# Whole output columns in the last four weight blocks of the first experts, and sums of squares by a matrix of ones

## The chip, the cores and the metric

The kernel runs on one core of one Trainium2 chip. The metric is the device time of one execution in microseconds (us). In the profile PE is the engine of the matmuls and PEld its weight loads, DVE, ACT and POOL are the vector, scalar and GpSimd engines, and SP is the engine that issues the DMAs. All data are 32-bit floats.

## What is computed

The reference is a block with a gated linear attention, a long convolution and a mixture of 16 experts, and two further layers behind it. The part around the change is the end of the first mixture of experts and the norm behind it:

```
hid = silu(xs @ w_gate) * (xs @ w_up)              # per expert, 32 slots of 1024
y   = (hid @ w_down) * vals
x   = x + mod_x[5] * zeros.at[idx].add(y)          # 256 rows of 1024
x   = x * rsqrt(mean(x * x, -1) + 1e-6) * norm_final_g
```

The result is the input of the first of the two further layers, which begins with projections `x @ w_in_2[0]`.

## The kernel before

The residual stream lies transposed in `X`: 8 rows (row here means `X[:, d, :]`), each of 128 channels on the partitions by 256 tokens. `T` is a scratch tile of the same form. `ONES` is a 128x128 tile of ones that the kernel already has.

The 16 experts run in four groups of four, x = 0 to 3. For each group the weights of the four experts come as blocks of 2 MB, each 128 partitions by 4096 values, in an order that the tensor program writes out (`weights(...)` appends to `order`). SP runs through that order: it waits for the last matmul that read the block's slot (`finished`), and issues the DMA into it. The PE waits for a block with `arrived`. In the stretch around the change eight blocks of a group's w_down are read: 4 for output columns 0 to 511 (half 0) and 4 for columns 512 to 1023 (half 1).

`four_experts` (line 979 and on) computes one half: block `part` holds 256 of the 1024 hidden rows for all 512 columns of the half, so each of the four blocks adds 2 steps of `kk` for each of four experts, and the bank with the result is whole only after the fourth block. The matmul of line 996 has 32 columns of weights (the slots of one expert), and the four experts write different 32-partition strips of one bank. The trace shows two PE instructions for each such call, 16 for a block.

Then, for half 1 of the last group, in this order:

- ACT copies the bank, 128x512, to `YE` (line 2851).
- `combine(3, 2)` and `combine(3, 3)` (line 1059): the PE multiplies `YE` by `PVT`, which puts the slots back to their tokens with their weights; two rows of `X` per call.
- DVE adds them to `X` (line 2032), row by row.
- ACT squares two rows at once into `T` (`final_squares`, line 2811).
- `squares(b)` (line 1067): the PE multiplies `T`, as the weights, by one column of ones and sums the squares of each token in bank `fsum`, as 128x2.
- ACT takes the root of 128x2 (line 2860), DVE the reciprocal (line 2073), and the PE turns it to 128x256, the same on each partition, by two transposes of a broadcast column (line 1112, recorded under line 645).
- DVE scales rows 0 to 3 of `X` (line 2079) and rows 4 to 7 (line 2083), reading the factor from the bank.
- The next layer's `kx` (line 1187) multiplies the eight rows as they come ready, 16 instructions, then `cq` and others go on from all of `X` (line 640).

Rows 0 to 3 of `X` are updated and squared earlier, while half 1 is loaded: `combine(3, 0)`, `combine(3, 1)`, `squares(0)` and `squares(1)` stand after half 0 in the PE's order.

`keep_on(n, ...)` (line 665) is n matmuls of 256 columns on constants whose result nobody reads; the trace shows two instructions for each. It stands ahead of parts 2 and 3 of half 1 (2 and 3 of them), ahead of the transposes (1), and ahead of `kx` (1).

`full(...)` and `out(...)` count a semaphore up, `wait_ge(*at(...))` waits for the count. `fresh(...)` takes the next of the 8 PSUM banks in turn.

Of the kernel before, what the change touches and what calls it, by code (L numbers as in the profile page):

```python
# [7 lines left out]
ALU = mybir.AluOpType  # L8
# [261 lines left out]
class Signals:  # L270
# [38 lines left out]
    def at(self, *key):  # L309
        if self.counting and key not in self.value:  # L310
            return None, 1
        return self.value[key]
# [72 lines left out]
def bc(ap, shape):  # L385
    return ap.to_broadcast(shape)
# [9 lines left out]
def program(nc, ring_d, ranked_d, p1_d, p2_d, pf_d, xT_d, cT_d, pos_d, out_d):  # L396
    order, slot_read = [], []
    with contextlib.ExitStack() as ctx:
# [6 lines left out]
        def bank(*key):  # L405
            return PS[:, banks.of[key], :]
# [15 lines left out]
        def p1(name, *dims):  # L422
            off, n = P1[name]
            return V(o1 + off, *(dims or (n,)))
# [190 lines left out]
        def tensor(g):  # L615
# [45 lines left out]
            def keep_on(n, *where, take=fresh, of=None):  # L661

                ps = take("idle", *where)
                for _ in range(n):
                    ins = g.matmul(ps[:, 0:256], *(of or (ident, V(o1, 256))), start=True, stop=True)  # L665
                ins.then_inc(*up("pe", "idle", *where))
# [314 lines left out]
            def four_experts(ps, key, done, rows_of, ready=None, ahead=((), (), (), ())):  # L981


                for part in range(4):
                    for q in ahead[part]:
                        first_slots(q)
                    w, i = weights(*key, part)
                    wv = w.rearrange("p k (e n) -> p k e n", e=4) if len(w.shape) == 3 else w.rearrange("p (k e n) -> p k e n", k=2, e=4)
                    if ready:
                        g.wait_ge(*at(*ready, part // 2 if ready[1] else part))  # L990
                    if done == ("ye", 3, 1) and part > 1:
                        keep_on((2, 3)[part - 2], "ye", part)
                    arrived(i)
                    for kk in (2 * part, 2 * part + 1):
                        for e in range(4):
                            ins = g.matmul(ps[32 * e:32 * e + 32, :], rows_of(kk, e), wv[:, kk % 2, e, :], start=kk == 0, stop=kk == 7)  # L996
                    ins.then_inc(*(full(*done) if part == 3 else up("pe")))
                    finished(i)
# [60 lines left out]
                    ins = g.matmul(ps[:, j * 256:(j + 1) * 256], YE[:, x, (2 * b + j) * 128:(2 * b + j + 1) * 128], PVT[:, x, :], start=True, stop=True)  # L1059
                ins.then_inc(*full("ex", x, b))  # L1060

            def squares(b):

                g.wait_ge(*at("fsq", b))
                for k in (2 * b, 2 * b + 1):
                    for ti in range(2):
                        ins = g.matmul(bank("fsum")[:, ti:ti + 1], T[:, k, ti * 128:(ti + 1) * 128], p1("one"),
                                       start=k == 0 and ti == 0, stop=k == 7, skip_group_check=True)
                return ins

            for x in range(4):
                for half in range(2):
                    for mat in range(2):
                        ps = fresh("gu", x, half, mat)
                        four_experts(ps, (("w_gate", "w_up")[mat], x, half), ("gu", x, half, mat),
                                     lambda kk, e: XS[x][:, kk, 32 * e:32 * e + 32], ("xs", x),
                                     ((), (), (), ()) if x or half or mat else ((0, 1), (2,), (3,), ()))
                    ps = fresh("hidt", x, half)
                    g.wait_ge(*at("gu", x, half, 1))
                    for j in range(4):  # L1080
                        ins = turn(ps[:, j * 128:(j + 1) * 128], SIL[half][:, j * 128:(j + 1) * 128])
                    ins.then_inc(*full("hidt", x, half))
                    if x < 2:
                        routing_sums(x, half)
                    if x and half == 0:
                        for b in range(4):
                            combine(x - 1, b)
                if x < 3:
                    slots(x + 1)
                weights_turned(x)  # L1090
                g.wait_ge(*at("hidt", x, 1))
                for half in range(2):
                    ps = fresh("ye", x, half)
                    four_experts(ps, ("w_down", x, half), ("ye", x, half), lambda kk, e: HIDT[:, kk, 32 * e:32 * e + 32])
                    if x == 3 and half == 0:
                        combine(3, 0)
                        combine(3, 1)
                        fresh("fsum")
                        banks.hold("fsum")
                        squares(0)  # L1100
                        squares(1)
            combine(3, 2)
            combine(3, 3)
            for b in (2, 3):
                ins = squares(b)
            ins.then_inc(*full("fsum"))
            banks.release("fsum")
            keep_on(1, "fstd")
            ps = fresh("fstd")
            g.wait_ge(*at("frs"))  # L1110
            for ti in range(2):
                ins = turn(ps[:, ti * 128:(ti + 1) * 128], bc(RS1[:, ti:ti + 1], [128, 128]))
            ins.then_inc(*full("fstd"))
            note("pe", "moe_end", "pe")

            for l in range(2):
# [534 lines left out]
        def vector(v):  # L1651
# [402 lines left out]
            for x in range(4):  # L2054
# [12 lines left out]
                        angles(2 * x + half - 3)  # L2067
                if x < 3:
                    slots(x + 1)
            for b in range(4):  # L2070
                combine(3, b)
            v.wait_ge(*at("fstd"))
            v.reciprocal(RS1, MS1).then_inc(*out("frs"))
            full("fstd")
            rstd = bank("fstd")[:, 0:256]
            for b in range(2):
                rows = X[:, 2 * b:2 * b + 2, :]
                v.wait_ge(*at("fg", b))
                v.tensor_tensor(rows, rows, bc(rstd.rearrange("p (o t) -> p o t", o=1), [128, 2, 256]), ALU.mult).then_inc(*out("x", 0, 2 * b))
                note("dve", "x", 0, 2 * b + 1)  # L2080
            for k in range(4, 8):
                v.wait_ge(*at("fsq", k // 2))
                v.scalar_tensor_tensor(out=X[:, k, :], in0=X[:, k, :], scalar=p1("g_fin")[:, k:k + 1], in1=rstd, op0=ALU.mult, op1=ALU.mult) \
                    .then_inc(*out("x", 0, k))
            note("dve", "fstd_read")
            note("dve", "moe_end", "dve")
            sig.stage = "m0"

# [514 lines left out]
        def scalar(s):  # L2603
# [225 lines left out]
            for x in range(4):  # L2829
                for half in range(2):  # L2830
                    full("gu", x, half, 0)
                    if x:
                        full("hidt", x - 1, half)
                    if (x, half) == (1, 0):
                        s.wait_ge(*at("read", SLOTS.index(HM_SLOT)))
                        s.dma_start(posi, bass.AP(tensor=pos_d.tensor, offset=pos_d.offset, ap=[[0, 128], [1, 256]])).then_inc(*land("in9", "pos_in"))
                    s.activation(SIL[half], bank("gu", x, half, 0), ACT.Silu, bias=0.0, scale=1.0).then_inc(*out("gu", x, half, 0))
                    full("hidt", x, half)
                    if x:
                        full("ye", x - 1, 1)  # L2840
                    s.activation(HIDT[:, half * 4:half * 4 + 4, :], bank("hidt", x, half).rearrange("p (j s) -> p j s", j=4), ACT.Copy) \
                        .then_inc(*out("hidt", x, half))
                    if (x, half) in ((1, 1), (2, 0), (2, 1)):
                        sines(2 * x + half - 3)
                if x < 3:
                    slots(x + 1)
                full("pvt", x)
                s.activation(PVT[:, x, :], bank("pvt", x)[:, 0:256], ACT.Copy).then_inc(*out("pvt", x))
                for half in range(2):
                    full("ye", x, half)  # L2850
                    s.activation(YE[:, x, half * 512:(half + 1) * 512], bank("ye", x, half), ACT.Copy).then_inc(*out("ye", x, half))
                    if x == 3 and half == 0:
                        settle()
                        s.activation(STAT[:, 62:63], EPS5, ACT.Sqrt, bias=0.0, scale=1.0).then_inc(*out())
                        final_squares(0)
                        final_squares(1)
            final_squares(2)
            final_squares(3)
            full("fsum")
            s.activation(MS1, bank("fsum")[:, 0:2], ACT.Sqrt, bias=EPS6, scale=1.0 / 1024).then_inc(*out("fsum"))  # L2860
            note("act", "fstd")
            note("act", "moe_end", "act")

            for l in range(2):
# [505 lines left out]
def layout(i, order):  # L3370
# [9 lines left out]
    def block(key):  # L3380
# [9 lines left out]
            return part(n["w_out"][0], a[0])  # L3390
        if kind in ("w_gate", "w_up", "w_down"):
            x, half, q = a
            w = n[kind][0, 4 * x:4 * x + 4, 256 * q:256 * q + 256, 512 * half:512 * half + 512]
            return w.reshape(4, 2, 128, 512).transpose(2, 1, 0, 3).reshape(128, -1)
        l = a[0]
# [89 lines left out]
```

## Time and profile before

| | us |
|---|---|
| median of 3 runs (lowest, highest) | 1627.51 (1626.91, 1627.9) |
| the profiled execution, time | 1627.17 |
| its span from the first to the last instruction | 1625.4 |
| PE busy in the span | 1407.9 |
| DVE busy | 509.0 |
| ACT busy | 314.1 |
| first experts' weights, line 996: matmuls busy | 237.7 |
| idle of the PE before line 996, for DMA | 135.0 |

Times in rows are microseconds from the start of the span, unless marked ns. A row of the time line has the start, the length, the engine, the line in the kernel, what is done with the sizes and how many instructions were merged, and in square brackets how long the engine was idle before it and what it waited for. Neighbouring rows of different engines overlap. A matmul's recorded length includes its way through the array, so matmuls that follow each other overlap too. PEclk is the clock granted to the PE: 1.00 is 2.4 GHz, 0.50 is 1.2 GHz.

### The profile page before, as it was taken

To read this page: it belongs to the slowest core of one execution; us is meant where nothing else is said; L and a number is where in the kernel's file an instruction comes from. 1 tells how busy PE (TensorE), PEld (TensorE's weight loads), DVE (VectorE), ACT (ScalarE), POOL (GpSimd) and SP (SyncE) were. 2 spreads that over 40 slices of the span, in tenths; PEclk is the share of its full clock that TensorE was granted. 3 is DMA by queue.
4 is the path that set the end of the run, shared out by engine and by line. 5 is a ranking of instruction groups with operands and counts; after the bars stand their busy time and mean duration, and the time that the engine had idled before them with its cause. 6 is when DMAs were issued, how large, how long until landed. Compare 5 with 4: busy or idle time off the path is not lost. (4 is left out here: it accounts for less than half of the span.)

```text
span 1625.4 us, 19345 instructions
## 1 busy us (share of the span) xinstructions
PE 1407.9 (87%) x7684; PEld 789.8 (49%) x7684; DVE 509.0 (31%) x1140; ACT 314.1 (19%) x659; POOL 0.2 (0%) x4
## 2 busy tenths in 40 slices
PE   6999999856656566599999999997999989999978
PEld 4665877412311211166777644432667677444424
DVE  5225553101101101015763522221346744232213
ACT  2422202100000100112332312211223223122202
POOL 0000000000000000000000000000000000000000
PEclk9999999978877878899999999999999999999999
DMA  9465477999999999992321599999715214899993
GB/s 387 167 251 209 165 293 316 412 429 427 427 428 427 428 427 429 427 422 81 145 104 52 216 380 399 411 417 412 315 52 207 98 59 156 345 406 416 418 412 152
DMA packets 56386, 492.62 MB, mean 303 GB/s; under 512 B 6240, under 2 KB 6624, under 8 KB 25952
## 3 DMA queue, kind: packets, MB, share of 16 engines
q1 hardware_dynamic: 56144, 491.15, 74.0%
q8 instruction: 66, 1.08, 0.3%
q14 instruction: 32, 0.26, 0.0%
q10 hardware_dynamic: 144, 0.13, 0.0%
HBM read 490.21 MB, written 1.05 MB: 302 GB/s over the span
## 5 line engine op out<-in xcount | busy, mean ns | idle before, releaser
L640 PE MATMUL PS<-A 128*128 128x256 f32 (+6 forms) x1592 | 376.6, 393 | 5.3 <-ACT A L2624 1.5
L996 PE MATMUL PS<-A 128*32 128x512 f32 x1536 | 237.7, 757 | 135.0 <-DMA A<-ring_d 135.0
L640 PEld LDWEIGHTS PS<-A 128*128 128x128 f32 (+1 forms) x1592 | 277.9, 193 | 96.9 <-issue 57.3
L996 PEld LDWEIGHTS PS<-A 128*32 128x32 f32 x1536 | 52.7, 126 | 306.4 <-issue 238.5
L1528 PE MATMUL PS<-A 128*64 128x512 f32 (+1 forms) x1024 | 188.6, 608 | 12.5 <-DMA A<-ranked_d 12.2
L1528 PEld LDWEIGHTS PS<-A 128*64 128x64 f32 (+1 forms) x1024 | 57.1, 128 | 126.4 <-issue 124.6
L2058 DVE TENSOR_TENSOR A<-A,PS 128x512 f32<-128x512 f32 x8 | 5.5, 687 | 321.0 <-PE PS L996 321.0
L1557 PE MATMUL PS<-A 128*64 128x512 f32 (+1 forms) x512 | 94.9, 597 | 6.7 <-issue 4.7
L645 PE MATMUL PS<-A 128*128 128x128 f32 (+1 forms) x444 | 66.1, 279 | 17.8 <-DVE A L2058 7.1
L645 PEld LDWEIGHTS PS<-A 128*128 128x128 f32 (+1 forms) x444 | 50.0, 143 | 60.4 <-issue 36.0
L2509 DVE TENSOR_TENSOR A<-A,PS 128x256 f32<-128x256 f32 x26 | 11.0, 423 | 194.3 <-ACT A L3059 194.3
L1557 PEld LDWEIGHTS PS<-A 128*64 128x64 f32 (+1 forms) x512 | 27.4, 126 | 70.4 <-issue 66.1
L1391 PE MATMUL PS<-A 128*128 128x256 f32 x256 | 59.3, 383 | 2.3 <-DVE A L2323 1.2
L1391 PEld LDWEIGHTS PS<-A 128*128 128x128 f32 x256 | 47.5, 190 | 11.3 <-issue 3.9
L2515 DVE COPY A<-PS 128x512 f32<-128x512 f32 x26 | 18.0, 692 | 108.3 <-PE PS L1557 108.3
L1574 PE MATMUL PS<-A 128*128 128x512 f32 x104 | 49.5, 597 | 1.8 <-issue 1.8
L3059 ACT ACTIVATE A<-PS 128x256 f32<-128x256 f32 x26 | 10.0, 386 | 204.7 <-PE PS L1528 204.7
L1508 PE MATMUL PS<-A 128*128 128x256 f32 (+1 forms) x256 | 49.3, 343 | 0.0
L1508 PEld LDWEIGHTS PS<-A 128*128 128x128 f32 x256 | 41.0, 190 | 15.0 <-issue 11.4
L665 PE MATMUL PS<-A 128*128 128x256 f32 x156 | 37.5, 389 | 0.0
L2973 ACT ACTIVATE A<-A 128x128 f32<-128x128 f32 (+1 forms) x48 | 21.2, 443 | 73.4 <-DVE A L2285 73.4
L2504 DVE TENSOR_SCALAR A<-PS,A 128x256 f32<-128x256 f32 (+1 forms) x64 | 28.6, 489 | 18.3 <-PE PS L1508 17.6
(360 smaller groups left out, 1302.8 us busy)
## 6 DMA issues: line engine op xcount, KB each, us to landing
A<-ring_d SPq DMA_DIRECT2D x156, 2048.0 KB, 26.6
A<-ranked_d SPq DMA_DIRECT2D x72, 1024.0 KB, 14.2
A<-ranked_d SPq DMA_DIRECT2D x144, 512.0 KB, 15.1
A<-ring_d SPq DMA_DIRECT2D x2, 1312.0 KB, 22.1
A<-ring_d SPq DMA_DIRECT2D x2, 1280.0 KB, 25.2
A<-p_d SPq DMA_DIRECT2D x1, 1232.0 KB, 22.5
A<-xT_d SPq DMA_DIRECT2D x1, 1024.0 KB, 5.5
A<-cT_d SPq DMA_DIRECT2D x1, 1024.0 KB, 12.0
```

The costliest lines, as they stand in the source:

```text
L640: ins = g.matmul(out, l, r, start=n == 0, stop=n == len(pairs) - 1)
L645: return g.transpose(out, in_, ident[0:k, 0:k])
L665: ins = g.matmul(ps[:, 0:256], *(of or (ident, V(o1, 256))), start=True, stop=True)
L996: ins = g.matmul(ps[32 * e:32 * e + 32, :], rows_of(kk, e), wv[:, kk % 2, e, :], start=kk == 0, stop=kk == 7)
L1391: ins = g.matmul(bank("wo", l, b)[:, j * 256:(j + 1) * 256], w[:, k, c:c + 128], O[:, k, :], start=k == 0 and j == 0, stop=k == 7, skip_gr ...
L1508: ins = g.matmul(ps[:, c:c + w], XGT[:, x, d * 128:(d + 1) * 128], px, start=True, stop=True)
L1528: ins = g.matmul(ps[m * s:m * s + m, :], XS2[u % 2][:, kk, c:c + m], wv[:, kk % nk, s, :], start=kk == 0, stop=kk == 7)
L1557: ins = g.matmul(ps[m * s:m * s + m, :], HD[n % 2][:, f, m * s:m * s + m], wd[f][:, s, half * 512:(half + 1) * 512], start=f == 0, stop=f ...
L1574: ins = g.matmul(PS[:, b, :], QT[p % 2], YE2[p % 2][:, half * 512:(half + 1) * 512], start=n == 0, stop=last)
L2504: ins = v.tensor_scalar(XS2[u % 2][:, d, 0:w], bank("xs2", l, u, part, 1)[:, j * 256:j * 256 + w], gain, bias, ALU.mult, ALU.add)
L2515: v.tensor_copy(YE2[p % 2][:, 512:1024], bank("ye2", l, p, 1)).then_inc(*out("ye2", l, p, 1))
L2973: ins = s.activation(p, p, ACT.Exp, bias=ST[:, i, c:c + 1], scale=1.0, accum_out=ST[:, i, 4 + c:5 + c])
```

## The change

The last four blocks (w_down, x = 3, half 1) are cut another way: block q holds 128 output columns, 512 + 128q to 639 + 128q, for all 1024 hidden rows. So each block gives one whole row of `X`. `last_columns(q)` does, on the PE: 8 steps of `kk` for four experts with 128 columns, then the combine of this one row, then the sum of its squares, before the next block. ACT copies 128x128 and squares one row, DVE adds one row.

The sums of squares, for all rows, are made with `ONES` as the weights and the squares as the 256 columns. The sum is thus on every partition, 128x256; ACT takes the root of all of it into `T[:, 0, :]`, DVE takes the reciprocal of all of it in place, and the two transposes are gone. The `keep_on` at the end has 3 in place of 1 and stands behind the sum.

```diff
-                    if done == ("ye", 3, 1) and part > 1:
-                        keep_on((2, 3)[part - 2], "ye", part)
...
+            def squares(rows, *key):
+
+                g.wait_ge(*at("fsq", *key))
+                for k in rows:
+                    ins = g.matmul(bank("fsum")[:, 0:256], ONES, T[:, k, :], start=k == 0, stop=k == 7)
                 return ins
+
+            def last_columns(q):
+
+                w, i = weights("w_down", 3, 1, q)
+                wv = w.rearrange("p (k e n) -> p k e n", k=8, e=4)
+                ps = fresh("ye", 3, 1, q)
+                if q > 1:
+                    keep_on((2, 3)[q - 2], "ye", q)
+                arrived(i)
+                for kk in range(8):
+                    for e in range(4):
+                        ins = g.matmul(ps[32 * e:32 * e + 32, 0:128], HIDT[:, kk, 32 * e:32 * e + 32], wv[:, kk, e, :], start=kk == 0, stop=kk == 7)
+                ins.then_inc(*full("ye", 3, 1, q))
+                finished(i)
+                ps = fresh("ex", 3, 4 + q, "row")
+                g.wait_ge(*at("ye", 3, 1, q))
+                g.matmul(ps[:, 0:256], YE[:, 3, (4 + q) * 128:(5 + q) * 128], PVT[:, 3, :], start=True, stop=True).then_inc(*full("ex", 3, 4 + q, "row"))
+                return squares((4 + q,), 4 + q, "row")
...
-            combine(3, 2)
-            combine(3, 3)
-            for b in (2, 3):
-                ins = squares(b)
+            for q in range(4):
+                ins = last_columns(q)
             ins.then_inc(*full("fsum"))
             banks.release("fsum")
-            keep_on(1, "fstd")
-            ps = fresh("fstd")
-            g.wait_ge(*at("frs"))
-            for ti in range(2):
-                ins = turn(ps[:, ti * 128:(ti + 1) * 128], bc(RS1[:, ti:ti + 1], [128, 128]))
-            ins.then_inc(*full("fstd"))
+            keep_on(3, "fstd")
...
-            for b in range(4):
+            for b in range(2):
                 combine(3, b)
-            v.wait_ge(*at("fstd"))
-            v.reciprocal(RS1, MS1).then_inc(*out("frs"))
-            full("fstd")
-            rstd = bank("fstd")[:, 0:256]
+            for d in range(4, 8):
+                full("ex", 3, d, "row")
+                v.scalar_tensor_tensor(out=X[:, d, :], in0=bank("ex", 3, d, "row")[:, 0:256], scalar=MA[:, 7, d:d + 1],
+                                       in1=X[:, d, :], op0=ALU.mult, op1=ALU.add).then_inc(*out("ex", 3, d, "row"))
+            v.wait_ge(*at("fsum"))
+            rstd = T[:, 0, :]
+            v.reciprocal(rstd, rstd).then_inc(*out())
+            settle()
...
-            final_squares(2)
-            final_squares(3)
+            for q in range(4):
+                d = 4 + q
+                full("ye", 3, 1, q)
+                s.activation(YE[:, 3, d * 128:(d + 1) * 128], bank("ye", 3, 1, q)[:, 0:128], ACT.Copy).then_inc(*out("ye", 3, 1, q))
+                s.wait_ge(*at("ex", 3, d, "row"))
+                s.activation(T[:, d, :], X[:, d, :], ACT.Square, bias=0.0, scale=1.0).then_inc(*out("fsq", d, "row"))
             full("fsum")
-            s.activation(MS1, bank("fsum")[:, 0:2], ACT.Sqrt, bias=EPS6, scale=1.0 / 1024).then_inc(*out("fsum"))
+            s.activation(T[:, 0, :], bank("fsum")[:, 0:256], ACT.Sqrt, bias=EPS6, scale=1.0 / 1024).then_inc(*out("fsum"))
```

Left out of the diff above: `squares(0)` and `squares(1)` become `squares((0, 1), 0)` and `squares((2, 3), 1)`, the loops over `half` leave out half 1 of the last group, DVE's scaling of rows 4 to 7 waits for the squares row by row, and `layout` packs the four blocks in their new form, of the same size.

## Rows read from the trace of the kernel before

**Rows 1.** Table of stretches, first experts: busy us per engine, PEclk, DMA share, GB/s

```profile
600.00:700.00 100.00, 64.19 (x388) 19.94 (x381) 6.58 (x14) 7.71 (x14) 0.00 (x0) 0.83 1.01 427
```

**Rows 2.** Time line from the last block's landing into the next layer

```profile
701.52 1.92 PE L996 MATMUL PS<-A 128*32 128x512 f32 x16 [0.36 <-DMA A<-ring_d]
...
703.51 0.60 ACT L2851 ACTIVATE A<-PS 128x512 f32<-128x512 f32 x1 [12.19 <-PE PS L996]
...
704.21 1.97 PE L1059 MATMUL PS<-A 128*128 128x256 f32 x8 [0.76 <-ACT A L2851]
705.35 1.74 DVE L2032 SCALAR_TENSOR_TENSOR A<-PS,A 128x256 f32<-128x256 f32 x4 [16.23 <-PE PS L1059]
706.26 0.63 ACT L2811 ACTIVATE A<-A 128x512 f32<-128x512 f32 x1 [2.15 <-DVE A L2032]
...
706.94 1.95 PE L1067 MATMUL PS<-A 128*128 128x1 f32 x16 [0.77 <-ACT A L2811]
...
708.92 0.26 ACT L2860 ACTIVATE A<-PS,A 128x2 f32<-128x2 f32 x1 [1.17 <-PE PS L1067]
709.22 0.17 DVE L2073 RECIPROCAL A<-A 128x2 f32<-128x2 f32 x1 [2.13 <-ACT A L2860]
...
709.53 0.66 PE L645 MATMUL PS<-A 128*128 128x128 f32 x2
...
710.23 1.28 DVE L2079 TENSOR_TENSOR A<-A,PS 128x512 f32<-128x512 f32 x2 [0.84 <-PE PS L645]
...
711.06 4.42 PE L1187 MATMUL PS<-A 128*128 128x256 f32 x16
...
715.31 17.43 PE L640 MATMUL PS<-A 128*128 128x256 f32 x80
```

**Rows 3.** Time line from squares(1) to the block before the last

```profile
689.77 0.61 ACT L2811 ACTIVATE A<-A 128x512 f32<-128x512 f32 x1
...
690.44 1.05 PE L1067 MATMUL PS<-A 128*128 128x1 f32 x8 [0.35 <-ACT A L2811]
...
691.42 5.34 PE L996 MATMUL PS<-A 128*32 128x512 f32 x32
...
696.69 1.13 PE L665 MATMUL PS<-A 128*128 128x256 f32 x4
...
697.75 1.92 PE L996 MATMUL PS<-A 128*32 128x512 f32 x16
...
699.60 1.56 PE L665 MATMUL PS<-A 128*128 128x256 f32 x6
```

**Rows 4.** Time line of the next layer's norms, which sum with a matrix of ones

```profile
733.64 0.47 ACT L2619 ACTIVATE A<-PS,A 128x256 f32<-128x256 f32 x1 [0.27 <-PE PS L652]
...
734.02 0.41 ACT L2615 ACTIVATE A<-A 128x256 f32<-128x256 f32 x1
...
734.25 1.75 DVE L2176 RECIPROCAL A<-A 128x256 f32<-128x256 f32 x1 [21.17 <-ACT A L2619]
...
734.59 0.70 PE L652 MATMUL PS<-A 128*128 128x256 f32 x2
735.22 0.67 PE L1222 MATMUL PS<-A 32*96 32x256 f32 x2
```

**Rows 5.** Groups by form (count, busy us, mean ns, idle), and line 861's time line

```profile
L3067 ACT ACTIVATE A<-PS 128x128 f32<-128x128 f32 x26 | 7.1, 272 | 0.0
...
L996 PEld LDWEIGHTS PS<-A 128*32 128x32 f32 x1536 | 52.7, 126 | 306.4 <-issue 238.5 <-DMA A<-ring_d 56.7 <-ACT A L2837 8.9
...
82.44 1.10 PE L861 MATMUL PS<-A 64*64 64x128 f32 x32
```

**Rows 6.** A block at the low clock, and stretches with the granted clock (third from the end)

```profile
613.47 3.62 PE L996 MATMUL PS<-A 128*32 128x512 f32 x16 [2.97 <-DMA A<-ring_d]
...
692.00:696.00 4.00, 4.00 (x28) 1.00 (x21) 0.00 (x0) 0.00 (x0) 0.00 (x0) 0.57 1.03 430
709.00:712.00 3.00, 2.98 (x8) 1.68 (x8) 1.94 (x5) 0.19 (x1) 0.00 (x0) 0.52 0.97 409
```

More of the change, by code:

```diff
@@ L1060, in combine @@
                 ins.then_inc(*full("ex", x, b))
-            def squares(b):
-                g.wait_ge(*at("fsq", b))
-                for k in (2 * b, 2 * b + 1):
-                    for ti in range(2):
-                        ins = g.matmul(bank("fsum")[:, ti:ti + 1], T[:, k, ti * 128:(ti + 1) * 128], p1("one"),
-                                       start=k == 0 and ti == 0, stop=k == 7, skip_group_check=True)
-                return ins
+            def squares(rows, *key):
+                g.wait_ge(*at("fsq", *key))
+                for k in rows:
+                    ins = g.matmul(bank("fsum")[:, 0:256], ONES, T[:, k, :], start=k == 0, stop=k == 7)
+                return ins
+            def last_columns(q):
[14 more added lines that the diff above has]
+                return squares((4 + q,), 4 + q, "row")
             for x in range(4):
@@ L1091, in tensor @@
                 g.wait_ge(*at("hidt", x, 1))
-                for half in range(2):
+                for half in range(2 if x < 3 else 1):
                     ps = fresh("ye", x, half)
@@ L1099, in tensor @@
                         banks.hold("fsum")
-                        squares(0)
-                        squares(1)
-            combine(3, 2)
-            combine(3, 3)
-            for b in (2, 3):
-                ins = squares(b)
+                        squares((0, 1), 0)
+                        squares((2, 3), 1)
+            for q in range(4):
+                ins = last_columns(q)
             ins.then_inc(*full("fsum"))
             banks.release("fsum")
-            keep_on(1, "fstd")
-            ps = fresh("fstd")
-            g.wait_ge(*at("frs"))
-            for ti in range(2):
-                ins = turn(ps[:, ti * 128:(ti + 1) * 128], bc(RS1[:, ti:ti + 1], [128, 128]))
-            ins.then_inc(*full("fstd"))
+            keep_on(3, "fstd")
             note("pe", "moe_end", "pe")
@@ L2081, in vector @@
             for k in range(4, 8):
-                v.wait_ge(*at("fsq", k // 2))
+                v.wait_ge(*at("fsq", k, "row"))
                 v.scalar_tensor_tensor(out=X[:, k, :], in0=X[:, k, :], scalar=p1("g_fin")[:, k:k + 1], in1=rstd, op0=ALU.mult, op1=ALU.mult) \
                     .then_inc(*out("x", 0, k))
-            note("dve", "fstd_read")
             note("dve", "moe_end", "dve")
@@ L2848, in scalar @@
                 s.activation(PVT[:, x, :], bank("pvt", x)[:, 0:256], ACT.Copy).then_inc(*out("pvt", x))
-                for half in range(2):
+                for half in range(2 if x < 3 else 1):
                     full("ye", x, half)
@@ L2856, in scalar @@
                         final_squares(1)
-            final_squares(2)
-            final_squares(3)
+            for q in range(4):
[4 more added lines that the diff above has]
+                s.activation(T[:, d, :], X[:, d, :], ACT.Square, bias=0.0, scale=1.0).then_inc(*out("fsq", d, "row"))
             full("fsum")
-            s.activation(MS1, bank("fsum")[:, 0:2], ACT.Sqrt, bias=EPS6, scale=1.0 / 1024).then_inc(*out("fsum"))
-            note("act", "fstd")
+            s.activation(T[:, 0, :], bank("fsum")[:, 0:256], ACT.Sqrt, bias=EPS6, scale=1.0 / 1024).then_inc(*out("fsum"))
             note("act", "moe_end", "act")
@@ L3392, in block @@
             x, half, q = a
+            if (kind, x, half) == ("w_down", 3, 1):
+                w = n[kind][0, 12:16, :, 512 + 128 * q:640 + 128 * q]
+                return w.reshape(4, 8, 128, 128).transpose(2, 1, 0, 3).reshape(128, -1)
             w = n[kind][0, 4 * x:4 * x + 4, 256 * q:256 * q + 256, 512 * half:512 * half + 512]
```

## The prediction, made before the changed kernel was run

> **What bounds the kernel now.** I read the table of stretches first. Through the first experts the DMA engines are busy all the time at 427 GB/s while the PE is busy 64 of 100 us [rows 1]: a block of 2.10 MB lands every 2.10/0.427 = 4.9 us, and that sets the pace. The last block that matters here (part 3 of w_down for the last four experts) lands at 701.5, where the PE starts on it [rows 2]. From there the chain is serial, and the time line gives it: matmuls to 703.44, copy of YE from 703.51, combine from 704.21, update of X from 705.35, squares from 706.26, sums from 706.94 to 708.89, root, reciprocal, two transposes, and the first scaling of X at 710.23. The next layer's first projection (line 1187) follows at 711.06, and its next matmuls (line 640) at 715.31; these run without a gap, 80 in 17.43 us (0.218 each) [rows 2]. No matmul there waits for a block. So the PE bounds what follows, and every microsecond by which line 640 starts later is a microsecond of the kernel. I therefore compare one number: 715.31 before, and what it becomes.
>
> **What does not change.** The four blocks have the same bytes and the same order in the DMA queue, so they land at about 686.8, 691.7, 696.6 and 701.5 (701.5 less 4.9 each). Their slots are freed some microseconds later, but SP has transfers queued far ahead and none of the waiting work is next in line; I cost that at nothing, and at the same shift as the PE's if it showed.
>
> **The four blocks, in a row of waits.** Before, part 0 to 3 of the second half accumulated into one bank, and the PE waited only for landings. Now each block q holds 128 whole output columns, and before the PE may touch block q+1 it waits, in its own order, for ACT's copy of YE, then for DVE's update of X and ACT's square. Everything behind these two waits on the PE stands still: the next block's matmuls, which have landed, and in the end line 1187. One such round:
> - Matmuls: 32 calls give 64 instructions of 32x128 weights and 128 columns, in 16 groups of four that run side by side. Line 861 also runs four side by side with 128 columns: 32 in 1.10 us [rows 5]. That is 8 groups, 0.11 for each further one with a tail of 0.27, so 16 groups take 1.10 + 8 x 0.11 = 1.98. Before it was 1.92 per block [rows 2, 3].
> - Handover to ACT 0.07 (703.44 to 703.51), copy 128x128 0.27 [rows 5] where it was 0.60, handover to the PE 0.10 (704.11 to 704.21): 0.44.
> - Combine of one row, two instructions of 256 columns: 0.67 to 0.70, as line 652 [rows 4]. I take 0.67.
> - DVE: 0.04 handover and 0.48, the spacing in the row of 4 (1.74) being 0.42 and the last a whole one [rows 2]: 0.52.
> - ACT: 0.02 and a square of 128x256, 0.41 as at line 2615 [rows 4]; 0.05 to the PE: 0.48.
> The first matmul of the sum with ones thus starts 1.98 + 0.44 + 0.67 + 0.52 + 0.48 = 4.09 after the block's first matmul. The next block may follow 0.63 later, as line 1222 follows line 652 (734.59 to 735.22) [rows 4]: a round is c = 4.7 us.
>
> **Where the rounds lie.** squares(1) can start at 690.44 as before; it now has 4 instructions of 256 columns, which hold the PE 1.06 as keep_on of 4 did (696.69 to 697.75) [rows 3]. So block 0 starts at 691.5 (before 691.42), block 1 at 696.2, and its round ends at 700.9. keep_on(2) stands ahead of block 2: 1.06, start at 702.0. Round to 706.7, keep_on(3) 1.5 [rows 3], block 3 starts at 708.2, though it landed at 701.5. Each round fits under a landing (4.7 against 4.9), but the start at 691.5 is already 4.7 behind the first landing, and nothing gives that back: the two keep_on, which ran in waiting time before, now add 2.5.
>
> **The tail.** The sum starts at 708.2 + 4.1 = 712.3 and is done at 713.0 (0.67); before it was 708.89, so 4.1 later. Then ACT's root on 128x256: 0.04 + 0.47 [rows 4], where it was 0.03 + 0.26 on 128x2 [rows 2]. The reciprocal on 128x256 takes 1.75 and starts 0.14 after the root [rows 4], where it took 0.17 on 128x2. The two transposes and their handovers (709.39 to 710.23, 0.84) are gone, 0.04 stands for them. X is first scaled at 713.0 + 0.5 + 0.14 + 1.75 + 0.04 = 715.4, which is 5.2 later than 710.23. The scaling itself (1.28 for rows 0 to 3) stays.
> Something comes back in the projection. Before, its 16 instructions took 4.25 (711.06 to 715.31), because the granted clock was 0.52 from 709 to 712 [rows 6], after the PE had run 16 matmuls of one column (1.95 us) [rows 2]. The new sums have 256 columns each, and 6 + 2 instructions of keep_on stand right ahead of the projection, in its wait. I take the full clock, 2.4 GHz: 16 x 0.218 = 3.49, 0.76 less. keep_on itself (8 instructions, about 2 us) lies under the root and the reciprocal and costs nothing; without that cover it would cost its 2 us.
> Sum: 5.2 - 0.76 = +4.4. The profiled execution took 1627.17 with a span of 1625.4, which becomes 1631.6; from the median, 1627.51, it is 1631.9. I say 1631.7.
>
> **What the trace of before cannot show.** (1) Narrow weights with 128 columns on all 128 rows: from 1.9 (15 x 0.11 + 0.27, no start-up) to 4 x 1.8 = 7 if nothing ran side by side; nearest is line 861, so 2.0. (2) Handovers: each of the eight in a round is 0.02 to 0.14 in the rows; 0.03 more on each is 0.24 a round, 1.0 in all; as much less is no more than 0.4. (3) The number of banks taken changes from 7 to 11, so later steps meet other banks; between -0.5 and +0.5. (4) The clock, below. Together, at full clock, the shift is between +2.9 and +5.5.
>
> **Rivals.**
> - *The PE falls to 1.2 GHz in the rounds.* For it: in a round the PE's matmuls fill 1.8 + 0.4 + 0.4 = 2.6 of 4.7 us, with two holes of about 1 us, and the level has fallen in this trace behind blocks that use 1.9 of 4.9 [rows 6]. Against it: the sums and combines fall into the holes. A block took 3.62 at the low level against 1.92 [rows 2, 6], so each fall costs 1.7 while the PE is the one that is waited for. One or two falls: +6.1 to +7.8, 1633.3 to 1635.0.
> - *The weight loads come onto the path.* 64 loads instead of 16 per block. Line 996's mean 126 ns each, and before they lie beside matmuls of 512 columns, four times as long [rows 5]. If each of the 16 groups had to wait for its loads, 16 x 0.11 = 1.8 a round, 7 in all: 1638.6. Against it: line 861 has loads as often, and a group every 0.11. The Trainium skill (TensorE: Matmul & The Clock Gate, What overlaps and what doesn't) says that a load overlaps running matmuls only in another row group; here all four share every row, so by that rule this rival would hold. The trace disagrees so far: on line 996 with the same row groups 16 matmuls and their loads took 1.92.
> - *The rounds hide under the landings, and the change gains.* The place is the start of block 3. If 691.5 + 3c + 2.5 were no later than 701.5, which is c below 2.5, the tail after the last landing alone would count: 701.5 + 4.1 + 0.7 + 0.5 + 0.14 + 1.75 + 0.04 = 708.7, 1.5 earlier, and 0.76 from the clock: -2.3, 1624.9. The shift crosses zero at c = 3.6. For it: copy, combine and update of the last block are each smaller than before. Against it: of 4.7 only the matmuls' 2.0 are not measured at this very shape.
> - *The shift is swallowed behind.* If a block of the next layer were waited for, part of the 4.4 would vanish: 1627.5 to 1630. The 80 matmuls without a gap speak against it.
>
> **How the numbers follow.** Chances: forecast 0.63 (its own range 1630.1 to 1632.7), lower clock 0.16, loads on the path 0.04, hidden under the landings or nearly so 0.09, swallowed 0.08. The range 1629.0 to 1635.8 takes in the lower clock and part of the swallowed case, and leaves out the loads and the hidden rounds. About 0.2% (3.3 us) is what a measurement can tell from no change. Slower by more is c above 4.4 with nothing swallowed: most of the forecast (0.52) and the next two cases, 0.72. Within: 0.25. Faster by over 0.2% needs more than even the hidden case gives: 0.03.
>
> **What the profile after would show.** Blocks 0 to 3 starting near 691.5, 696.2, 702.0 and 708.2, with the PE idle in front of combine and sums and waiting for ACT, not for DMA; a reciprocal of 1.75 at 713.6; X first scaled at 715.4; the projection at full clock, and line 640's run from 719.7. I am wrong if block 3 starts as it lands, if a round is not 4.7, or if a gap of the PE before 740 shrinks by what the rounds added.

## The result and the profile after

The changed kernel takes 1633.66 us (median of 7, 1632.6 to 1635.43), the kernel before 1627.51 (7 runs here, 1623.94 to 1629.26). The ratio is 1.004, interval 1.003 to 1.0049: slower by 0.4%, where 1631.7 had been forecast. 1633.66 lies inside the stated range (1629.0 to 1635.8), but 1.0 above the forecast's own range (1630.1 to 1632.7), in the part that was given to the lower clock. The profiled execution took 1634.81, with a span of 1633.0.

The time line of the changed kernel, in the stretch of [rows 2, 3]:

```profile
687.67 3.75 PE L1057 MATMUL PS<-A 128*128 128x256 f32 x8 [0.76 <-issue]
...
691.44 2.75 PE L1064 MATMUL PS<-A 128*128 128x256 f32 x8
...
694.11 1.95 PE L1077 MATMUL PS<-A 128*32 128x128 f32 x64
...
696.13 0.28 ACT L2870 ACTIVATE A<-PS 128x128 f32<-128x128 f32 x1 [2.19 <-PE PS L1077]
...
696.56 0.67 PE L1082 MATMUL PS<-A 128*128 128x256 f32 x2 [0.49 <-ACT A L2870]
697.26 0.48 DVE L2081 SCALAR_TENSOR_TENSOR A<-PS,A 128x256 f32<-128x256 f32 x1 [4.93 <-PE PS L1082]
697.78 0.42 ACT L2872 ACTIVATE A<-A 128x256 f32<-128x256 f32 x1 [1.37 <-DVE A L2081]
...
698.25 0.70 PE L1064 MATMUL PS<-A 128*128 128x256 f32 x2 [1.03 <-ACT A L2872]
...
698.88 1.95 PE L1077 MATMUL PS<-A 128*32 128x128 f32 x64
...
703.55 1.03 PE L665 MATMUL PS<-A 128*128 128x256 f32 x4
...
704.51 1.96 PE L1077 MATMUL PS<-A 128*32 128x128 f32 x64
...
709.18 1.46 PE L665 MATMUL PS<-A 128*128 128x256 f32 x6
...
710.57 1.95 PE L1077 MATMUL PS<-A 128*32 128x128 f32 x64
...
714.71 0.70 PE L1064 MATMUL PS<-A 128*128 128x256 f32 x2 [1.02 <-ACT A L2872]
...
715.25 1.89 PE L665 MATMUL PS<-A 128*128 128x256 f32 x8
715.45 0.47 ACT L2874 ACTIVATE A<-PS,A 128x256 f32<-128x256 f32 x1 [0.79 <-PE PS L1064]
715.95 1.75 DVE L2085 RECIPROCAL A<-A 128x256 f32<-128x256 f32 x1 [1.75 <-ACT A L2874]
717.74 1.29 DVE L2090 TENSOR_TENSOR A<-A 128x512 f32<-128x512 f32 x2
...
718.58 3.69 PE L1194 MATMUL PS<-A 128*128 128x256 f32 x16 [1.44 <-DVE A L2090]
```

Line 1077 is a block's matmuls, 1082 its combine, 1064 its sum. Read one round from 694.11 to 698.88: the PE works 1.95, stands 0.49 for ACT's copy, works 0.67, stands 1.03 for DVE and ACT, works 0.70, and only then takes the next block, which had landed long before. None of the four blocks waits for a DMA any more; before, the last one did [rows 2].

For all that follows I measure one distance: from the start of the last block of half 0, which the PE begins as it lands, to the start of line 640's run. What happened before that landing is thereby left out.

```profile
683.27 3.64 PE L994 MATMUL PS<-A 128*32 128x512 f32 x16 [1.75 <-DMA A<-ring_d]
...
722.11 17.43 PE L640 MATMUL PS<-A 128*128 128x256 f32 x80
```

That is 38.84 in the changed kernel. Before, the same block stood in this row, and line 640's run at 715.31 [rows 2]:

```profile
681.94 3.53 PE L996 MATMUL PS<-A 128*32 128x512 f32 x16 [2.97 <-DMA A<-ring_d]
```

That is 33.37. So of the 7.6 us by which the two spans differ, 1.3 lie ahead of this landing, in work that the change does not touch, 5.5 in the stretch, and 0.8 behind. Just behind line 640 the shift stays as it is: line 652, at 734.59 before [rows 4], is at 741.39, the same 6.8 later as line 640.

```profile
741.39 0.70 PE L652 MATMUL PS<-A 128*128 128x256 f32 x2
```

### The profile page after: what moved, and what is told of

Read it like the earlier page. It is cut to its first block and busy times, and to the rows that moved or that the text cites. A ratio compares the mean times of both kernels' runs of the same rounds, so it can differ in the third digit from the quotient of the medians.

```text
span 1633.0 us, 19710 instructions
## 1 busy us (share of the span) xinstructions
PE 1405.5 (86%) x7862; PEld 793.7 (49%) x7862; DVE 510.9 (31%) x1140; ACT 315.5 (19%) x664; POOL 0.2 (0%) x4
## 5 line engine op out<-in xcount | busy, mean ns | idle before, releaser
L994 PE MATMUL PS<-A 128*32 128x512 f32 x1472 | 222.1, 739 | 142.8 <-DMA A<-ring_d 142.8
L1564 PEld LDWEIGHTS PS<-A 128*64 128x64 f32 (+1 forms) x512 | 27.4, 126 | 67.4 <-issue 64.9
```

Of the source, the lines that this page charges most:

```text
L1564: ins = g.matmul(ps[m * s:m * s + m, :], HD[n % 2][:, f, m * s:m * s + m], wd[f][:, s, half * 512:(half + 1) * 512], start=f == 0, stop=f ...
```

## What was tried

All runs in one table; the distance is from the one profile of each, so every distance is a single execution, while a ratio is from 5 to 13 of them.

| kernel | ratio to before | interval | distance, us |
|---|---|---|---|
| before | | | 33.4 |
| before, again | 1.0012 | 1.0001 to 1.0022 | 35.9 |
| changed | 1.004 | 1.003 to 1.0049 | 38.8 |
| changed, again | 1.0034 | 1.0021 to 1.0046 | 37.5 |
| changed, no keep_on in the rounds | 1.0 | 0.9989 to 1.0011 | 36.7 |
| columns alone | 1.0044 | 1.003 to 1.0057 | 39.9 |
| matrix of ones alone | 1.002 | 1.0009 to 1.003 | 33.7 |
| changed, keep_on before | 1.0035 | 1.0023 to 1.0047 | 35.9 |
| the same, again | 1.0026 | 1.0017 to 1.0036 | 37.4 |
| next block first | 0.9989 | 0.9979 to 1.0 | 31.8 |
| next block first, old sums | 0.9997 | 0.9984 to 1.0011 | 32.4 |
| row, then next block | 0.9992 | 0.9982 to 1.0001 | 31.3 |
| row, then next block, old sums | 0.9998 | 0.9983 to 1.0013 | 30.5 |
| row, then next block, keep_on before | 0.9992 | 0.9977 to 1.0007 | 31.5 |

The kernel before, measured against itself, came out at 1.0012. So differences of 0.1% between two ratios carry nothing here, and the reasons below rest on the distances first. The distances leave something out, too: over the 14 profiles the landing that they start from lies between 680.8 and 686.2 us, and what follows the start of line 640 takes 908.6 to 913.4 us, with no order by kernel. A distance can therefore show where time goes in this stretch, but a profile's distance and a kernel's median need not differ by the same amount.

### The changed kernel without the keep_on in the rounds

```diff
-                if q > 1:
-                    keep_on((2, 3)[q - 2], "ye", q)
```

> The changed kernel without the two keep_on ahead of its blocks 2 and 3. Theory A (the four rounds run one behind the other on the PE, and all that stands between them is on the path): blocks 2 and 3 start 1.1 and 2.6 us earlier against block 0, the distance from the last landing-paced block of half 0 to line 640 falls from 38.8 to about 36.3 us, and the time from 1633.7 to about 1631.1. Theory B (the granted clock is what costs, and the keep_on hold it up): the clock falls to 0.5 within the rounds, a block's matmuls take 3.6 instead of 1.95 us at least once, and the time stays at 1633 or above.

Its four blocks:

```profile
696.81 1.95 PE L1075 MATMUL PS<-A 128*32 128x128 f32 x64
...
701.58 1.95 PE L1075 MATMUL PS<-A 128*32 128x128 f32 x64
...
706.35 1.96 PE L1075 MATMUL PS<-A 128*32 128x128 f32 x64
...
711.12 1.95 PE L1075 MATMUL PS<-A 128*32 128x128 f32 x64
```

4.77 apart, each at the full clock. The distance is from these two rows:

```profile
685.97 3.64 PE L994 MATMUL PS<-A 128*32 128x512 f32 x16 [1.81 <-DMA A<-ring_d]
...
722.65 17.43 PE L640 MATMUL PS<-A 128*128 128x256 f32 x80
```

It is 36.68, 2.2 less than in the changed kernel, which had the same start of block 0 (10.84 behind the landing in both). Theory A holds for the distance (36.3 expected), B does not in this profile: two `keep_on` that before ran while the PE waited for a landing cost 0.9 and 1.3 us once nothing waits for a landing.

The time fell by more than that: the median is 1629.42, where 1631.1 had been expected, and the ratio went from 1.004 to 1.0, which is about 6 us. The distance accounts for 2.2 of them and is still 3.3 above that of before. What the rest is stays open; the profiled execution was the slowest of the 13 (1638.09), so its spans outside the stretch can't tell.

### Each half of the change alone

Columns alone: `squares` with the one column of ones, root and reciprocal on 128x2, the transposes and one `keep_on` at the end instead of three, as before the change, inside the changed kernel.

```diff
-                    ins = g.matmul(bank("fsum")[:, 0:256], ONES, T[:, k, :], start=k == 0, stop=k == 7)
+                    for ti in range(2):
+                        ins = g.matmul(bank("fsum")[:, ti:ti + 1], T[:, k, ti * 128:(ti + 1) * 128], p1("one"),
+                                       start=k == 0 and ti == 0, stop=k == 7, skip_group_check=True)
```

> Whole columns in the last four blocks as in the changed kernel, but the sums by one column of ones, root and reciprocal on 128x2 and the two transposes as before the change. Theory A (the rounds cost most of it): rounds of 4.7 us as in the changed kernel, 4.1 us later at the end of the sums than before; the tail to the first scaling is 1.3 us instead of 2.5, the projection gives back nothing if the clock falls behind the one-column matmuls. About 1631.5 to 1633. Rival R (root and reciprocal over 256 columns are the larger part): within 1 us of before, 1627.5 to 1628.5.

Ones alone: the same lines the other way, in the kernel before.

> The kernel before with the matrix of ones alone: blocks as before, sums as 128x256, root and reciprocal over 256 columns, no transposes, three keep_on. Theory A: the tail is 1.1 us longer, and the projection is 0.8 us shorter at the full clock: within 1 us of before, about 1627.8. Rival R: most of the 6 us are here, 1631 or above.

With the matrix of ones alone the distance is 33.7, 0.3 from before, as the sum had it: from the first of the last sums to the scaling it takes 4.3 instead of 3.3, and the projection is shorter by 0.7. Its time is another matter: the median is 1630.45 where 1627.8 was expected, and the ratio of 1.002 (1.0009 to 1.003) means 1.5 to 4.9 us. In its profile 2.4 us more than before lie behind line 640, where the kernels are alike; the kernel before came out at 1.0012 of itself, so I don't read a cost of the ones from it, but the times don't rule one out. Rival R falls on the distance, and with it the thought that the reciprocal over 256 columns is the larger part.

Columns alone is as slow as the whole change, with a median of 1634.9 (1631.5 to 1633 expected) and a distance of 39.9, although its tail is the short one (713.87 to 715.81). The rounds show why, in the matmuls of blocks 0 and 2:

```profile
690.35 3.20 PE L1079 MATMUL PS<-A 128*32 128x128 f32 x64
...
702.86 2.74 PE L1079 MATMUL PS<-A 128*32 128x128 f32 x64
```

3.20 and 2.74 instead of 1.95: the granted clock was at 1.2 GHz for part of each, and again for the projection (4.44). So the rival of the falling clock, which I had put against the changed kernel, is what happens in this profile without the matrix of ones. In the changed kernel's two profiles the rounds ran at 2.4 GHz throughout. One profile of columns alone can't say how often, but the other profiles point the same way. Where the clock was full ahead of the first sums, it fell to half in the block behind them in all four profiles with one column of ones (before, columns alone, and the two orders with old sums below), and in none of the seven with the matrix of ones.

### keep_on ahead of the rounds, and both kernels again

```diff
+                    if done == ("ye", 3, 0) and part > 1:
+                        keep_on((2, 3)[part - 2], "ye0", part)
                     arrived(i)
```

> The changed kernel with keep_on(2) and keep_on(3) also ahead of parts 2 and 3 of the half before, where the PE waits for landings. Theory C (block 0's start now sets the end, so a low clock in the combines and sums ahead of it, which the profiled run showed at 0.50 until 692.6, costs about 1.2 us that the landings hid before): the combines and sums run at the full clock, block 0 starts 9.5 us after the last landing-paced block instead of 10.8, and the time is about 1 us less, 1632.6. If the extra over the forecast lies elsewhere: 1633.7, unchanged.

> The changed kernel once more, for a second profile. Theory C (what precedes block 0 is now on the path, and the clock there differs from run to run): the distance from the last landing-paced block of half 0 to line 640 is 35.9 us if that block, the combines and the sums run at the full clock, up to 38.8 if they run at half, and what follows block 0 is the same to 0.1 us if the clock is full there. Otherwise 38.8 again.

> The kernel before once more, for a second profile. Theory C: whatever clock the combines and sums get, the distance from the last landing-paced block of half 0 to line 640 stays within 0.5 us of 33.4, since block 3's landing sets it; only the projection's clock behind it can take or give 0.8 us. The time is that of before.

> The changed kernel with the keep_on ahead of the half before, once more: its first profile had the full clock from the last landing-paced block on and a distance of 35.9 us to line 640, but its median was not below the changed kernel's by more than the noise. If the keep_on hold the clock in each run, 35.9 to 36.0 again and the median 1 to 3 us under the changed kernel's 1633.7. If it was luck, the clock is at half in part of the block, the combines or the sums, and the distance is 37 to 39.

In four profiles of the changed form block 0 starts at very different distances behind the landing: 7.9 with the keep_on before (both profiles), 9.5 in the changed kernel again, 10.8 in its first profile. These are the three cases of the clock: full from the landing on, half in the last block of half 0, half in that block, through the combines and into the sums. In the first profile eight matmuls of the combines took 3.75 (above), in the second 1.97:

```profile
680.97 3.48 PE L994 MATMUL PS<-A 128*32 128x512 f32 x16 [2.98 <-DMA A<-ring_d]
685.23 1.97 PE L1057 MATMUL PS<-A 128*128 128x256 f32 x8 [0.77 <-issue]
...
690.48 1.95 PE L1077 MATMUL PS<-A 128*32 128x128 f32 x64
...
718.48 17.43 PE L640 MATMUL PS<-A 128*128 128x256 f32 x80
```

From block 0 to line 640 it is 28.00 in both. So the changed kernel hands on whatever the clock does ahead of block 0, 2.9 us between the best and the worst case. Half of my expectation fell, though: the kernel before is not immune. Its second profile had the low clock from 684 to 696 without a break:

```profile
684.00:696.00 12.00, 11.22 (x48) 6.78 (x44) 1.75 (x4) 5.15 (x9) 0.00 (x0) 0.50 1.00 426
```

and its time line has the landing, the last block and line 640:

```profile
683.13 3.64 PE L996 MATMUL PS<-A 128*32 128x512 f32 x16 [1.84 <-DMA A<-ring_d]
...
705.00 1.93 PE L996 MATMUL PS<-A 128*32 128x512 f32 x16
...
719.00 17.43 PE L640 MATMUL PS<-A 128*128 128x256 f32 x80
```

The last block started 21.9 behind the landing instead of 19.6, without waiting for its own landing, and the distance is 35.9, where 33.4 give or take 0.5 had been expected. So the two second profiles differ by only 1.6 (37.5 and 35.9), the two first by 5.5. The landings hide a low clock in the kernel before only until their slack is used up, 0.36 us in the first profile [rows 2] and 1.50 with the matrix of ones alone, where the clock was full from the combines on.

With the keep_on before, the clock was full from the landing up to block 0 both times, and block 0 started 7.9 behind the landing where 9.5 had been expected. The same holds for the third profile with them (the last run in the table), and for only two of the eleven profiles without them, so they seem to hold the clock there. But in the second profile it fell behind the first round, in block 1, and most of the gain was gone (37.4, of 35.9 at best):

```profile
691.38 1.95 PE L1079 MATMUL PS<-A 128*32 128x128 f32 x64
...
696.15 3.44 PE L1079 MATMUL PS<-A 128*32 128x128 f32 x64
```

So a fall within the rounds does occur with the matrix of ones too, in one of the five profiles of serial rounds with it. It costs 1.5 (3.44 for 1.95). The two medians are 1633.34 and 1633.11, where 1632.6 and then 1 to 3 us under 1633.7 had been expected; the ratios, 1.0035 and 1.0026, can't be told from the changed kernel's 1.004 and 1.0034. Whether these keep_on help on average stays open.

### Another order on the PE

```diff
-            for q in range(4):
-                ins = last_columns(q)
+            last_columns(0)
+            last_columns(1)
+            last_row(0)
+            last_columns(2)
+            last_row(1)
+            last_squares(0)
+            keep_on(1, "ye", 3)
+            last_squares(1)
+            last_row(2)
+            last_columns(3)
+            last_squares(2)
+            last_row(3)
+            ins = last_squares(3)
```

`last_columns` is here the matmuls of a block alone, `last_row` its combine, `last_squares` its sum; the two keep_on of the rounds are left out. ACT's and DVE's programs are untouched.

> The changed kernel with another order on the PE: the next block's matmuls stand ahead of the waits for the block before (block 0, block 1, row 0, block 2, row 1, sum 0, one keep_on, sum 1, row 2, block 3, sum 2, row 3, sum 3). Theory A (only the order makes the rounds serial): block 3 starts as it lands, 19.6 us after the last landing-paced block of half 0, the distance from that block to line 640 is about 31.1 us (33.4 before, 38.8 changed), and the time about 2 us below that of before. If ACT and DVE rather than the PE's order hold the rounds: block 3 still starts 3 us or more late.

> As the run with the next block first, but the sums by one column, root and reciprocal on 128x2 and the two transposes. The tail from the last sum to the first scaling is 1.3 us instead of 2.5; the clock may fall to 0.5 behind the one-column matmuls and take 0.8 us of the projection. Distance to line 640 between 30.0 (full clock) and 31.0 us; time 2 to 3 us below that of before.

The distance is 31.8 (31.1 expected), 7.0 below the changed kernel's first profile and 5.7 below its second, and 1.6 below before. Part of the 7.0 is the clock ahead of block 0, which starts 9.5 behind the landing here and 10.8 there. From block 0 to line 640 it is 28.0 in the changed kernel, 25.8 without the two keep_on and 22.3 here: the keep_on are 2.2 of the 7.0, the order is 3.5, and the clock ahead of block 0 is 1.4. The matmuls of a block now fill the waits of the block before. Block 3 starts 20.25 behind the landing, not 19.6, for two reasons that its rows show: row 2's combine at 700.96 stands just ahead of it, and block 1 had a gap.

```profile
681.23 3.46 PE L994 MATMUL PS<-A 128*32 128x512 f32 x16 [2.98 <-DMA A<-ring_d]
...
690.71 3.68 PE L1077 MATMUL PS<-A 128*32 128x128 f32 x122
...
695.84 0.42 PE L1077 MATMUL PS<-A 128*32 128x128 f32 x6 [1.44 <-issue]
...
700.96 0.59 PE L1085 MATMUL PS<-A 128*128 128x256 f32 x2
701.48 1.95 PE L1077 MATMUL PS<-A 128*32 128x128 f32 x64
...
713.02 17.43 PE L640 MATMUL PS<-A 128*128 128x256 f32 x80
```

The PE had nothing to wait for that the time line shows, and six matmuls of a block came 1.44 late. Three of the four other runs with a new order have the same kind of gap, at 0.2 to 0.3. The trace's records of single DMA packets have a candidate: in each of these four runs a packet of 16 KB of the kind "instruction" ends 1.3 to 1.5 us before the gap does (at 694.39 in this run, with the gap over at 695.84). The PE may have been short of instructions, then; no run tests it, and the cause stays open.

With the old sums the tail is 0.9 shorter (X first scaled 26.5 behind the landing instead of 27.4), but the clock fell to half behind the one-column matmuls and the projection gave it back: 32.4, where 30.0 to 31.0 had been expected. The time missed its expectation too: at 0.9997 it is that of before, not 2 to 3 us less.

Against that order, the next one moves each row's combine ahead of the next block, and its sum behind it:

```diff
             last_columns(0)
-            last_columns(1)
             last_row(0)
-            last_columns(2)
-            last_row(1)
+            last_columns(1)
             last_squares(0)
-            keep_on(1, "ye", 3)
+            last_row(1)
+            last_columns(2)
             last_squares(1)
             last_row(2)
+            keep_on(1, "ye", 3)
             last_columns(3)
```

> The changed kernel with each row's combine ahead of the next block and its sum behind the next block (block 0, row 0, block 1, sum 0, row 1, block 2, sum 1, row 2, one keep_on, block 3, sum 2, row 3, sum 3). In the run with the next block first, block 3 started 20.25 us after the last landing-paced block of half 0, 0.7 behind its landing, since row 2 came just ahead of it and block 1 had a gap of 1.44 us. Theory A: here block 3 starts at its landing, 19.6, and the distance to line 640 is 31.1 us; time 2 us or a little more below before. If the PE's gaps move with the order: 31.8 again.

> The same order with the sums by one column, root and reciprocal on 128x2 and the transposes, and one keep_on in the wait before the last sum. Tail 1.3 us instead of 2.5: X is first scaled 25.8 us after the last landing-paced block of half 0 (26.8 with the matrix of ones in this order). If the granted clock stays up, line 640 follows at 30.1; if it falls behind the one-column matmuls, at 30.9 to 31.7, no better than with the matrix of ones.

> The order of the run with each row ahead of the next block, with the keep_on ahead of parts 2 and 3 of the half before. Block 3 starts at its landing with or without them, since there is 2 us of cover by now: distance 31.1 to 31.4 and the time that of the run without them, 1626.5, or at most 1 us less where a long low clock would have used up the cover.

In this order the last block waits for its landing again, 19.67 behind the landing of half 0's last block:

```profile
705.84 2.11 PE L1077 MATMUL PS<-A 128*32 128x128 f32 x64 [1.36 <-DMA A<-ring_d]
```

The distance is 31.3 (31.1 expected), and 31.5 with the keep_on before, which buys nothing once there is cover. With the old sums and one keep_on in the wait before the last one, the clock held through tail and projection in this one profile and the distance is the shortest, 30.5 (30.1 expected), even though block 0 ran partly and block 1 wholly at half (2.50 and 3.64): there is room for that now. Its time does not show it: 0.9998 of before.

In time these versions are clearly faster than the changed kernel. Against before they are at 0.9989 to 0.9998, with intervals that touch 1: the three with the matrix of ones land 0.1% below, which is no more than the kernel before differs from itself. A gain of 1.6 to 2.0 us over the first profile of before is what the distances with the matrix of ones say, and not what the times can prove.

## Why the prediction held, point by point

- **The bound.** Held. Line 640's start set the rest: it and line 652 moved by the same 6.8.
- **The rounds are serial.** Held, and shown by the new order, which changes only the PE's program and takes 3.5 off the stretch from block 0 to line 640 of the kernel without keep_on in the rounds (22.3 for 25.8). A round was put at 4.7 and is 4.77; the first sum came 4.14 after its block's start (4.09); the next block 0.63 after it, as said.
- **Narrow weights.** Held: 64 loads and 64 matmuls take 1.95 (1.98). The rival of the loads is out. Line 861, which spoke against it in the prediction, has 64x64 tiles that take turns on two halves of the rows, so it could not have decided; the blocks' own row does. The Trainium skill's rule that a load overlaps running matmuls only in another row group (TensorE: Matmul & The Clock Gate, What overlaps and what doesn't) does not hold here: the four column strips share all rows, the loads' records fill 1.69 us of the same 1.95, and the measurement decides.
- **keep_on in the rounds.** Put at 1.06 and 1.5, measured 0.86 and 1.29 (5.63 and 6.06 between blocks, less 4.77). Slightly too dear: keep_on follows the sum after 0.53 (703.02 to 703.55) where a block follows after 0.63, and the block follows keep_on's start after 0.96, not 1.06.
- **The tail.** Put at 3.1 from the last sum's start to the scaling, measured 3.03 (714.71 to 717.74); reciprocal 1.75 as said, started 0.03 behind the root and not 0.14. The eight instructions of keep_on lie in its wait.
- **The projection at the full clock.** Held, 3.53 (3.49), in all profiles of the changed kernel.
- **From block 0 to line 640** that makes 28.0, forecast 28.2, before 23.9: 4.1 of the shift.
- **Where the sum was short.** It let block 0 start at 691.5, 0.1 from before, and so took its lead-up from one profile as if it were a fixed length. It is not: 7.9 to 10.8 behind the landing by the clock in the changed form, 9.5 in the first profile of before and 10.8 in the first one after. Before, the lead-up had a little cover (0.36 us in the first profile); the change took it away, and I had costed the clock within the rounds but not ahead of them. In the first profile that is 1.4 us of the 5.5. In the second the lead-up is 9.5, and the distance of 37.5 is within 0.3 of the forecast's 37.8.
- **The number.** The mechanism was right, but the time came out 6 us above before (1633.66 less 1627.51) and not 4.2, and the interval of that comparison (4.9 to 8.0 us) leaves the forecast out; the second one (1.0034, 3.4 to 7.5 us) takes it in. That the first landed within the stated range is owed to the room left for a lower clock, which did come, though ahead of the rounds and not in them. The lead-up is 1.4 us in one pair of profiles only, since the second profile of before has a long one as well (11.6); in that pair 1.3 more lie ahead of the stretch and 0.8 behind it. How much of the 6 us the lead-up is on average stays open.
- **The rival "hidden under the landings"** named the right quantity, block 3's start, and the wrong way to it: not a shorter round but an order in which rounds overlap. It gave -2.3; the new orders give -1.6 to -2.0 with the matrix of ones, and -1.0 and -2.9 with the old sums. Its crossing at c = 3.6 lets a shorter round shorten the last 4.1 as well, while its -2.3 keeps them; by the latter working the shift crosses zero at 3.2.
- **A count.** The prediction gives a round eight handovers; its own working lists five. Measured, a round came out at 4.77 for 4.7, so the allowance for them was not needed.

## What to carry to other kernels

Here, cutting transfers so that each gives a finished piece brought line 640 forward only where the engine that takes the next piece did not wait, in its own order, for the last piece to be finished. Put the next piece's work ahead of that wait. Work that is put into an engine's waiting time, keep_on as well as a stage that may run at the low clock, has to be costed again whenever a change removes the waiting. And a change that shortens a tail can pay in the step it substitutes: the reciprocal of 128x256 is 1.75 us, that of 128x2 is 0.17.

## What was not expected of the hardware

- The 32-wide weight strips: 64 pairs of load and matmul of 128 columns in 1.95 us, no slower than 16 pairs with 512 columns (1.92).
- A gap of 1.44 us within a run of 128 such matmuls, with no wait in the profile; open, with a packet of instructions that ends 1.45 us before the gap does as a candidate.
- In the block behind the first sums the clock fell to half in four of four profiles with one column of ones, and in none of seven with the matrix of ones (in one of them it fell a round later).
- The same kernel, run again, came out 0.12% slower than itself, with an interval that leaves out 1.
